# Attention scores in two row halves, and a swap of work between GpSimd and VectorE

## The reference, cut to what matters

```python
s = jnp.einsum('bqhmd,bkhmd->bhmqk', qblk, k) * scale      # two maps m, 64 values each
p = jax.nn.softmax(s, axis=-1)
a = p[:, :, 0] - lam * p[:, :, 1]
o = jnp.einsum('bhqk,bkhd->bqhd', a, v)                    # v: 128 values a head
```

## Time and profile before

| | us |
|---|---|
| median of 3 runs | 1243.48 |
| lowest and highest | 1238.59, 1243.86 |
| the profiled execution | 1243.99 |
| its span in the trace | 1242.2 |
| TensorE busy | 1104.3 (89%) |
| VectorE busy | 608.8 (49%) |
| ScalarE busy | 415.5 (33%) |
| GpSimd busy | 237.4 (19%) |

### The profile page before, as it was taken

One profiled execution on the slowest core, in us unless ns is written; L12 is line 12 of the kernel. 1 busy time (PEld: TensorE's weight loads), 2 busy tenths in 40 slices (PEclk: granted clock), 3 DMA queues, 4 the chain that ended last, 5 costly groups with the idle time before them and its releaser, 6 DMA issues. The chain is left out here.

```text
span 1242.2 us, 20824 instructions
## 1 busy us (share of the span) xinstructions
PE 1104.3 (89%) x7006; PEld 792.9 (64%) x7006; DVE 608.8 (49%) x1049; ACT 415.5 (33%) x831; POOL 237.4 (19%) x163
## 2 busy tenths in 40 slices
PE   4799999998999897889898799997799869799966
PEld 1587777766999886888888588886433213233332
DVE  0763545204565686777777456666133212233326
ACT  2651111113433673656557546631000000000013
POOL 0000000003000394457666100000110010010041
PEclk9799999998999998899999899997899889899988
DMA  9336676612110453550611343313968873768366
GB/s 363 126 136 236 225 243 226 198 66 70 27 35 1 114 125 107 102 140 18 158 35 51 88 154 105 117 69 122 369 230 281 271 271 120 256 209 265 123 228 262
DMA packets 127944, 196.96 MB, mean 159 GB/s; under 512 B 20592, under 2 KB 93200, under 8 KB 125790
## 3 DMA queue, kind: packets, MB, share of 16 engines
q1 hardware_dynamic: 98700, 144.39, 36.2%
q10 hardware_dynamic: 23378, 30.27, 7.0%
q0 software_dynamic: 5760, 20.97, 5.1%
HBM read 382.85 MB, written 39.24 MB: 340 GB/s over the span
## 5 line engine op out<-in xcount | busy, mean ns | idle before, releaser
L2186 PE MATMUL experts_gu_ps<-moe_wgu,experts_xT 128*32 128x512 f32 x1408 | 169.0, 618 | 22.4 <-DMA moe_wgu<-in_w_exp_up 13.9
L97 PE MATMUL proj_acc_ps<-proj_w_hi,hidden_hT_hi 128*128 128x512 f32 x288 | 117.5, 408 | 8.0 <-DVE hidden_hT_lo L92 8.0
L2186 PEld LDWEIGHTS experts_gu_ps<-moe_wgu,experts_xT 128*32 128x32 f32 x1408 | 43.6, 112 | 125.1 <-issue 96.4
L99 PE MATMUL proj_acc_ps<-proj_w_hi,hidden_hT_lo 128*128 128x512 f32 x288 | 115.3, 400 | 0.0
L98 PE MATMUL proj_acc_ps<-proj_w_lo,hidden_hT_hi 128*128 128x512 f32 x288 | 114.7, 398 | 0.0
L1323 POOL TENSOR_TENSOR att_e<-att_e 128x1152 f32<-128x1152 f32 (+1 forms) x36 | 86.0, 2389 | 73.0 <-DVE att_e L1403 73.0
L1341 ACT ACTIVATE att_e<-att_sc_ps,att_shift 128x1152 f32<-128x1152 f32 (+1 forms) x72 | 81.5, 1132 | 41.2 <-DVE att_shift L1392 41.0
L2207 PE MATMUL experts_y_ps<-moe_wd,experts_hidT 128*32 128x512 f32 x704 | 83.2, 614 | 9.2 <-issue 7.9
L1392 DVE TENSOR_REDUCE att_shift<-att_sc_ps 128x1 f32<-128x1152 f32 (+1 forms) x72 | 86.1, 1230 | 5.0 <-PE att_sc_ps L1437 5.0
L1466 PE MATMUL att_turned_ps<-att_in_v_tok,att_aT 128*128 128x128 f32 x584 | 77.2, 279 | 8.9 <-ACT att_aT L1349 8.9
L2156 POOL DMA_INDIRECT experts_xg<-scratch_h,all_step_token x22 | 30.5, 1386 | 260.9 <-PE experts_x_ps L2171 236.0
(11 more groups left out here) (380 smaller groups left out, 2156.5 us busy)
## 6 DMA issues: line engine op xcount, KB each, us to landing
moe_wgu<-in_w_exp_up ACTq DMA_DIRECT2D x356, 256.0 KB
moe_wgu<-in_w_exp_gate SPq DMA_DIRECT2D x356, 256.0 KB
moe_wd<-in_w_exp_down SPq DMA_DIRECT2D x89, 1024.0 KB
scratch_y_slots<-experts_y ACTq DMA_DIRECT2D x22, 512.0 KB, 5.7
proj_raw<-in_w_in SPq DMA_DIRECT2D x32, 256.0 KB, 5.4
proj_feat<-in_w_ada SPq DMA_DIRECT2D x4, 2048.0 KB, 8.3
proj_xh<-in_w_ada SPq DMA_DIRECT2D x4, 2048.0 KB, 9.3
proj_feat<-in_w_ada SPq DMA_DIRECT2D x4, 1024.0 KB, 5.9
```

What stands on the lines that cost most here:

```text
L97: pe.matmul(out, a_high, b_high, start=start, stop=False)
L99: return pe.matmul(out, a_low, b_high, start=False, stop=stop)
L2186: mm = pe.matmul(gu_ps[n % 2][at, :], xT[:, n % 2, k * P + c * Q:k * P + (c + 1) * Q], wgu[:, c, k], start=(k == 0), stop=(k == KT - 1))
```

## The change

Four things, in the diff below.

1. Scores. The low part's matmul now takes only the high queries, 64 rows: its low x low product is left out. `keys` holds three slabs (high of map 0, high of map 1, and one for low parts), and `queries` three (the two maps as before with the halves in the map's own order, and one that has the high queries on the other half). Map m has its own half of the 64 rows and the other one. After three full matmuls with the high keys, one per bank, come three of 64 rows with the low keys: bank m on the own half, bank 1-m on the other half, bank 2 on the own half. A prompt item does one full and one 64-row matmul for each map.
2. The scaling of the second map leaves VectorE's `scale_second` and becomes a multiply in GpSimd's `combine`, with a drain between it and the add. `scaled` is now raised by the ratio.
3. `split_w_out` is cut in two. GpSimd keeps the multiply and the cast and raises `w_out_high`; VectorE makes the low part of slice j in its round 11 + 3j, after both maxima.
4. `load_stack` issues eighteen DMAs a head instead of twelve; the low keys arrive in strips.

```diff
 def load_stack(sp, W, h):
+    keys, queries, done = W["keys"][h % 2], W["queries"][h % 2], W["stack_in"][h % 2]
     for m in range(2):
         rows = slice(m * QKD, (m + 1) * QKD)
-        for part, src in enumerate((W["k_high"], W["k_low"])):
-            for half in range(2):
-                sp.dma_start(W["keys"][h % 2][half * QKD:(half + 1) * QKD, m, part].bitcast(F32), src[h, rows, :]
-                             ).then_inc(W["stack_in"][h % 2], 16)
-        for half, src in enumerate((W["q_high"], W["q_low"])):
-            sp.dma_start(W["queries"][h % 2][half * QKD:(half + 1) * QKD, m].bitcast(F32), src[h, rows, :]
-                         ).then_inc(W["stack_in"][h % 2], 16)
+        own, other = (slice((m ^ half) * QKD, ((m ^ half) + 1) * QKD) for half in range(2))
+        banks = [slice(P + b * SCORES, P + (b + 1) * SCORES) for b in range(3)]
+        for half in (own, other):
+            sp.dma_start(keys[half, m].bitcast(F32), W["k_high"][h, rows, :]).then_inc(done, 16)
+        low = W["k_low"][h, rows, :]
+        for half, to, src in ((own, slice(0, P), slice(0, P)), (own, banks[0], banks[m]), (own, banks[1], banks[2]),
+                              (other, banks[2], banks[1 - m])):
+            sp.dma_start(keys[half, 2, to].bitcast(F32), low[:, src]).then_inc(done, 16)
+        for half, slab, src in ((own, m, "q_high"), (other, m, "q_low"), (other, 2, "q_high")):
+            sp.dma_start(queries[half, slab].bitcast(F32), W[src][h, rows, :]).then_inc(done, 16)
...
             def combine(it):
                 pool.wait_ge(scaled, it.n + 1)
-                pool.tensor_tensor(e[:, it.e, 0, 0:it.keys], e[:, it.e, 0, 0:it.keys], e[:, it.e, 1, 0:it.keys],
-                                   ALU.add).then_inc(a_done, 1)
+                first, second = (e[:, it.e, m, 0:it.keys] for m in range(2))
+                pool.tensor_scalar(second, second, ratio[:, it.n % 4:it.n % 4 + 1], None, ALU.mult)
+                pool.drain()
+                pool.tensor_tensor(first, first, second, ALU.add).then_inc(a_done, 1)
...
-                    split_w_out(pool, W, it.n - 8)
+                    split_w_out_high(pool, W, it.n - 8)
...
-                dve.tensor_scalar(ratio[:, r:r + 1], inv[:, r, 1:2], total[:, it.e, 0:1], lam_neg[:, 0:1], ALU.mult, ALU.mult)
-                dve.drain()
-                dve.tensor_scalar(e[:, it.e, 1, 0:it.keys], e[:, it.e, 1, 0:it.keys], ratio[:, r:r + 1], None,
+                dve.tensor_scalar(ratio[:, r:r + 1], inv[:, r, 1:2], total[:, it.e, 0:1], lam_neg[:, 0:1], ALU.mult,
                                   ALU.mult).then_inc(scaled, 1)
...
                     maximum(items[k], 1)
+                if k >= 11 and (k - 11) % 3 == 0 and (k - 11) // 3 < KT:
+                    split_w_out_low(dve, W, (k - 11) // 3)
...
-                q = queries[it.stack][:, m, it.t * P:(it.t + 1) * P]
-                for b in range(1 if it.prompt else 3):
-                    width = P if it.prompt else BANK
-                    cols = slice(it.first_key + b * BANK, it.first_key + b * BANK + width)
-                    out = sc[m][:, b * 512:b * 512 + width]
-                    pe.matmul(out, q, keys[it.stack][:, m, 0, cols], start=True, stop=False)
-                    mm = pe.matmul(out, q, keys[it.stack][:, m, 1, cols], start=False, stop=True)
-                mm.then_inc(sc_done[m], 1)
+                q, k = (stack[it.stack] for stack in (queries, keys))
+                at, own, other = slice(it.t * P, (it.t + 1) * P), slice(m * QKD, (m + 1) * QKD), slice((1 - m) * QKD, (2 - m) * QKD)
+                if it.prompt:
+                    out = sc[m][:, 0:P]
+                    pe.matmul(out, q[:, m, at], k[:, m, 0:P], start=True, stop=False)
+                    pe.matmul(out, q[own, m, at], k[own, 2, 0:P], start=False, stop=True).then_inc(sc_done[m], 1)
+                    return
+                banks = [sc[m][:, b * 512:b * 512 + BANK] for b in range(3)]
+                cols = [slice(P + b * BANK, P + (b + 1) * BANK) for b in range(3)]
+                for b in range(3):
+                    pe.matmul(banks[b], q[:, m, at], k[:, m, cols[b]], start=True, stop=False)
+                pe.matmul(banks[m], q[own, m, at], k[own, 2, cols[0]], start=False, stop=True)
+                pe.matmul(banks[1 - m], q[other, 2, at], k[other, 2, cols[2]], start=False, stop=True)
+                pe.matmul(banks[2], q[own, m, at], k[own, 2, cols[1]], start=False, stop=True).then_inc(sc_done[m], 1)
...
-def split_w_out(pool, W, step):
+def split_w_out_high(pool, W, step):
...
     elif step % 3 == 1:
         pool.drain()
-        pool.tensor_copy(W["w_out_hi"][:, k], raw[:])
-    else:
-        pool.drain()
-        split_low(pool, W["w_out_lo"][:, k], raw[:], W["w_out_hi"][:, k]).then_inc(W["w_out_split"], 1)
+        pool.tensor_copy(W["w_out_hi"][:, k], raw[:]).then_inc(W["w_out_high"], 1)
+
+
+def split_w_out_low(dve, W, k):
+
+    dve.wait_ge(W["w_out_high"], k + 1)
+    split_low(dve, W["w_out_lo"][:, k], W["w_out_raw"][:], W["w_out_hi"][:, k]).then_inc(W["w_out_split"], 1)
```

More of the change, by code:

```diff
@@ L1213, in _ @@
                     product(k + 2)
+SCORES = TILES * P // 3
+STACK_LOADS = 18
 class Item:
@@ L1256, in attention_stage @@
 def attention_stage(nc, I, C, W, M):
-    N, W_KEYS, BANK = HEADS * TILES, TILES * P, TILES * P // 3
+    N, W_KEYS, BANK = HEADS * TILES, TILES * P, SCORES
     items = [Item(n) for n in range(N)]
@@ L1265, in attention_stage @@
         lam_sum, lam_neg = s.sb("lam_sum", [P, 2]), s.sb("lam_neg", [P, 1])
-        W["keys"].append(s.sb("keys1", [P, 2, 2, (TILES + 1) * P], F32R))
-        W["queries"].append(s.sb("queries1", [P, 2, TILES * P], F32R))
+        W["keys"].append(s.sb("keys1", [P, 3, (TILES + 1) * P], F32R))
+        W["queries"].append(s.sb("queries1", [P, 3, TILES * P], F32R))
         keys, queries = W["keys"], W["queries"]
@@ L1427, in scores @@
                 if it.t == 0 and m == 0:
-                    pe.wait_ge(stack_in[it.stack], 16 * 12 * (it.head // 2 + 1))
+                    pe.wait_ge(stack_in[it.stack], 16 * STACK_LOADS * (it.head // 2 + 1))
                 if it.n >= 1:
                     pe.wait_ge(exp_done[m], it.n)
-                q = queries[it.stack][:, m, it.t * P:(it.t + 1) * P]
-                for b in range(1 if it.prompt else 3):
-                    width = P if it.prompt else BANK
-                    cols = slice(it.first_key + b * BANK, it.first_key + b * BANK + width)
-                    out = sc[m][:, b * 512:b * 512 + width]
-                    pe.matmul(out, q, keys[it.stack][:, m, 0, cols], start=True, stop=False)
-                    mm = pe.matmul(out, q, keys[it.stack][:, m, 1, cols], start=False, stop=True)
-                mm.then_inc(sc_done[m], 1)
+                q, k = (stack[it.stack] for stack in (queries, keys))
[12 more added lines that the diff above has]
+                pe.matmul(banks[2], q[own, m, at], k[own, 2, cols[1]], start=False, stop=True).then_inc(sc_done[m], 1)
             def turn(it, g):
@@ L2454, in build @@
                     W["v_tok"], W["v_in"] = right.sb("v_tok", [P, TILES + 1, 512], side="right"), [right.sem(f"v_in{h}") for h in range(HEADS)]
-                    W["keys"] = [right.sb("keys0", [P, 2, 2, (TILES + 1) * P], F32R, side="right")]
-                    W["queries"] = [right.sb("queries0", [P, 2, TILES * P], F32R, side="right")]
+                    W["keys"] = [right.sb("keys0", [P, 3, (TILES + 1) * P], F32R, side="right")]
+                    W["queries"] = [right.sb("queries0", [P, 3, TILES * P], F32R, side="right")]
                     W["lam_rows"], W["lam_in"] = right.sb("lam_rows", [P, 4, QKD], side="right"), right.sem("lam_in")
@@ L2462, in build @@
                 W["w_out_hi"], W["w_out_lo"] = m.sb("w_out_hi", [P, KT, D], F32R), m.sb("w_out_lo", [P, KT, D], F32R)
[L2463 removed]
+                W["w_out_in"], W["w_out_high"], W["w_out_split"] = m.sem("w_out_in"), m.sem("w_out_high"), m.sem("w_out_split")
                 with ExitStack() as raw_ctx:
```

## The result

The changed kernel is slower. Its median is 1283.72 us (1277.92 to 1313.76, four runs), that of the kernel before 1243.67 in runs beside it, the ratio 1.0316 with a 95% interval of 1.029 to 1.0343. One run, 1313.76, was disturbed and is not in the ratio. The profiled execution took 1277.92 us.

The account below looks back on a forecast made before the run. Attention was bound by a VectorE-ScalarE ring of 5.58 us, TensorE close behind at 5.20. Four heads gaining 1.8 each, less 0.7 and 0.45, gave 6.0 off 1243.99: 1238.0 us, own range 1232 to 1244, whole range 1226 to 1250.

Parts of the forecast that it names:

- GpSimd's multiply: Attention, second map on GpSimd: 1.27 us for 128x1152, priced from its 1126 ns multiply of 128x1024; upper bound 2.63.
- rival C: GpSimd becomes the bound with a multiply of 2.63: sixteen rounds at 6.5 instead of 5.6, 1252 us; chance 0.08.
- the ring: Attention round's loop of VectorE and ScalarE work without TensorE: 5.58 us, falling to 4.84 once the scaling leaves VectorE.
- That 0.38 is the only wait: TensorE's wait for ScalarE's copy before the last value passes; without it TensorE needs 5.20 of the 5.58 us round.
- handshake: 0.05 us added to each attention round for a delay that even a fed engine shows, giving 5.6.
- x = +0.18 a map: TensorE's scores: array shape changes and bare weight loads cost 0.355 us a map, less 0.175 saved by overlapping halves.
- Rival A: Array shape steps are cheaper, x near 0.03: rounds of 5.3 us, time 1228.6 us; chance 0.26.
- rival B: Halves don't overlap or the second pays its own load: 0.175 to 0.29 us a map more, 1249 to 1255; chance 0.16.
- 5.6 + 4.2 + 4.2: Head 1's rounds touched by the prompt item: one full round of 5.6 us and two short ones of 4.2.
- last sign: If the stages outside attention change by over 2 us, the sum's frame was wrong.
- Hidden too, by 0.4: VectorE's eight low parts, even when delayed by GpSimd's add, let the last copy land at 4.9, before TensorE's 5.3.
- SP's queue: Eighteen loads a head instead of twelve, 3.6 us more before the next output weight load; costed at 0, between 0 and 3.

Follow-up runs that it names:

- experiment 1: Changed kernel with GpSimd's multiply of the second map written as two operations (times ratio, times 1.0): 1239.45 us, 0.9984 of the kernel before.
- experiment 2: Kernel before with GpSimd's output-weight multiplies in other forms: four with one operation, 1240.96 us; then eight forms in one kernel, 1238.59 us.
- experiment 4: Kernel before with GpSimd scaling the second map in two operations and VectorE making the low parts, scores on all rows: 1235.21 us, 0.9958.
- experiment 6: Changed kernel with the two-operation multiply, a map's second half-row matmul moved to the same half as the first: 1254.03 us, 1.0130.
- experiment 7: Kernel before with GpSimd scaling the second map in two operations, the output weights' cast moved from GpSimd to ScalarE: 1234.65 us, 0.9933.

## Why the prediction was wrong, point by point

- **The failed step: GpSimd's multiply.** "The nearest row is its own multiply of 128x1024 by a column, 1126 ns, so 1.27 us for 1152." It took 3.20. The row was of the same engine and instruction name, but of another form: it had two operations, the new one has one. The kernel before has no GpSimd `tensor_scalar` with one operation, so its trace could not show the price. I set the bound at the add's 2.63, and rival C with it; the truth lay beyond both. Experiment 1 replaces the form and nothing else, and the loss is gone; experiment 2 shows about the same factor on other data.
- **What the price did.** With 3.20 a round has 5.96 us of GpSimd work, over the ring's 5.58 even where no output weights are handled, so every full item was hit and not the sixteen that C counted. With 5.96 to 7.2 us of work an item head 1 lost 60.79 - 49.38 = 11.4 us, and the mixer's start, behind all heads, 38.5 us. Rival C named the place and the sign rightly; its time, 1252, came from the too low price, and its chance of 0.08 from the same row.
- **VectorE and ScalarE.** The ring lost the scaling, as said. It was no longer the bound of a plain round in any kernel that had the swap; in rounds with its low part VectorE was (experiment 4).
- **TensorE.** 5.20 us a round was forecast for the old scores and 5.09 measured. "That 0.38 is the only wait" missed one: in the earlier trace rows the two passes at 587.85 start 0.21 apart (together they take 0.49), where a pass is 0.11, so 0.10 more was lost there. The 0.05 for a handshake stands in no row, and the rounds don't have it: 5.09 and twice 0.17 are 5.43. x = +0.18 a map was forecast, 0.17 measured (experiment 4 against 1), and its terms hold one by one. In experiment 1 the way in costs 0.09 over a step, the third half-row matmul 0.10, the way out 0.09, and the second transpose 0.06; the forecast has 0.095, 0.115, 0.095 and 0.05. The first two half-row matmuls start together, and the pair is worth 0.17 against 0.175. Rival A (cheap steps) and rival B (no overlap) are both refuted; B's lower price, 0.175 a map more, is what experiment 6 measured. The rule of the Trainium skill that I had weighed there, that a change of tiling mode drains TensorE (TensorEngine Tiling (Array Packing), Key Properties), is in line with it: 0.26 from the last full matmul to the first half one instead of 0.175.
- **The sum without the failed step.** The forecast of 1238.0 is about where experiment 1 came out, 1239.45, but that is partly luck: the forecast starts from 1243.99, and the kernel before had a median of 1240.61 beside experiment 1. The gain was 6.0 on paper and 2 measured, with an interval from none to 4. Plain rounds were shorter than said (5.43 for 5.6) and the head longer (48.57 for 47.6). The three rounds of head 1 that the prompt item touches took 5.21, 5.77 and 5.07, 16.05 in all where the sum has 5.6 + 4.2 + 4.2 = 14.0; the six others took 5.42 on average. The 5.77 is a round with VectorE's low part: without one on VectorE the same round takes 4.51 (experiment 7) and not 5.89 (experiment 4). By its own last sign, over 2 us outside attention, the sum's frame was wrong too; as said above, the stages behind vary by more than that with no change ahead of them.
- **VectorE's low parts.** That they would be long was foreseen from the earlier trace rows, by the exclusion of VectorE and GpSimd (the Trainium skill, SBUF — State Buffer, section SBUF: two separate sides); the trace agrees with 2.59 to 2.76 in experiment 4, each ending behind GpSimd's add, and in the changed kernel the other way round, with adds of 3.16 to 3.17. That it would be "Hidden too, by 0.4" was wrong for the kernel of experiment 4: the next product and maximum came late and with them the round, 6.35 for 5.09.
- **SP's queue.** No wait for the landing of keys or queries appears in the waits after; cost 0, as said.
- **The range.** Its upper end, 1250, lies even under rival C's 1252, and the nearest row was taken as the same thing. No row of the kernel before held an upper bound for the unseen form: GpSimd's add, the dearest of its instructions in this stage, is cheaper than the 3.20. The range had to be left wide for that, or the form tried alone first.

## What to carry to other kernels

When work moves to another engine, price it by a row of exactly that instruction form, operand for operand and operation for operation; a row that shares only the name is a guess, and the range has to say so. Work out how much of the new engine's round is then used: an engine that was at half load and gets 3.2 us more in a 5.6 us round sets the pace, and everything that the change does elsewhere no longer shows. Leave room, too, for what an engine's queue puts behind a new instruction: one low part of 2.6 us held back a ratio of 0.3. Half-row pairs for a small low part are not worth it here: one slot saved, two changes of the array's shape paid.

## What the runs showed of the hardware

- GpSimd's `tensor_scalar` with a single operation takes 2.5 times as long as with two: 3.20 against 1.23 us for 128x1152 (experiment 1), 2.77 to 3.47 against 1.05 to 1.19 for 128x1024 (experiment 2), for multiply and add, for a column and a constant, all in fp32 and in place. A second operation that does nothing (times 1.0) is the way to the fast one. Why the short form is slow, no run shows.
- Two matmuls of 64 rows on different halves and different banks start at the same time (530.04 both); on one half they start 0.27 apart, and the next one 0.18 behind (experiment 6).
- A change between full and half rows takes 0.26 from start to start where a step is 0.175, and the weight load of the first matmul behind it starts with the matmul (530.03). With both changes a map costs 0.17 us more, net of the slot that the pair saves (experiments 1 and 4).
- VectorE's subtract of two SBUF inputs, 1.23 us alone, took 2.59 to 2.76 in all eight cases of experiment 4, where GpSimd's add was already running, and ended 1.08 to 1.09 behind the add. In the changed kernel it was first, and all eight adds behind it took 3.16 to 3.17 instead of 2.64.
- That one pass of fp32r would be too coarse for the scores is the kernel's premise; no run here tried it.
